# Attention scores as three products over 64 rows for the two heads of a query tile, in place of two products over 128 rows for one head

## The chip, the cores and the metric

The kernel runs on one core of a Trainium2 chip. The metric is the device time of one execution in microseconds; less is better.

## The reference, cut to what matters

A two-layer encoder over 1,280 tokens (1,024 of one sequence, 256 of another), width 1,024, in float32. Each layer projects the normed input, mixes tokens in three ways, projects back, and runs a SwiGLU network. The change touches only the scores of the two attentions: six heads of 64 with a dilated mask over all keys of the sequence, and four heads of 64 with a neighbourhood window and a bias.

```python
qd = to_bhsd(rope(heads(q_d, N_DIL_HEADS), pos))        # dilated: 6 heads of 64
kd = to_bhsd(rope(heads(k_d, N_DIL_HEADS), pos))
...
scores = jnp.einsum('bhrnqe,bhrnke->bhrnqk', qr, kw,
                    preferred_element_type=jnp.float32) * (hd ** -0.5)
...
scores = jnp.einsum('bhrcqe,bhrcke->bhrcqk', qg, kg,    # neighbourhood: 4 heads of 64
                    preferred_element_type=jnp.float32) * (hd ** -0.5)
scores = scores + bias[None].astype(jnp.float32)
```

## The kernel before

Products are made in a rounded 32-bit format (fp32r). To keep float32 accuracy every operand is split into a high part, which is the value rounded, and a low part, which is the value less its high part. A product of two operands is then high by high, high by low and low by high (`products`, L1607 to L1609).

Each layer has five attention blocks of two heads (three dilated, `b` 0 to 2, then two of neighbourhood, `b` 3 and 4). A block first projects k, q and v for its two heads (128 columns: head 0 in partitions 0 to 63, head 1 in 64 to 127), in three chunks of 512, 512 and 256 tokens. VectorE takes k and q from PSUM into `TB` and `TA` (`drain`), in the dilated blocks ScalarE and VectorE rotate them (`swap`, `rope`), and then they are split: ScalarE writes the high parts (`split_k`, `split_q`), VectorE the low parts (`low_k`, `low_q`). Dilated blocks also project three convolution groups: the one named "c" before attention, drained by VectorE into `TA` only after the splits have been queued, and "h" and "b" in pieces between the steps of attention (`convolution`, units 0 to 11).

Because a head has only 64 rows and the array has 128, the kernel stacks the high part of a head's queries on its low part: `QS[0]` holds high in rows 0 to 63 and low in rows 64 to 127, `QS[1]` the reverse. `KH[h]` and `KL[h]` hold the head's keys, high and low, in both halves. Two products over 128 rows (L1720, L1721) then give all four partial products of a head. Writing both halves costs four pieces of 64 partitions per chunk for `KH`, four for `KL`, and two for each part of the queries.

The attention of a block runs over 20 units, two heads for each of ten query tiles of 128. A unit is a head, a query tile and `nkt` key tiles: 8 for the first sixteen units of a dilated block, 4 or 5 for those of a neighbourhood block, 2 for the last four of each. Its scores lie in two PSUM banks, `2 * (u % 2)` and the next. TensorE's program, in order: wait for the last splits and for the drain of the last projection, `scores(0)`, `scores(1)`, `turn_v`, and then for each unit `turn(u)` (transposes of the probabilities), `scores(u + 2)`, half of the convolution piece, `turn_y` after every second unit, the other half, and `values(u - 1)` (16 products of 128 columns for eight key tiles). VectorE adds the mask and takes the maximum (`mask`, L1317), ScalarE takes the exponential (`exp`, L893), and after `turn` they split the turned probabilities (`PTH`, `PTL`). The order on every engine is written out by hand; semaphores hold it together. The one that matters here is `s_masked`: `scores(u + 2)` writes the banks that `mask(u)` reads and waits for it.

Of the kernel before, what the change touches and what calls it, by code (L numbers as in the profile page):

```python
# [7 lines left out]
F32 = mybir.dt.float32  # L8
F32R = mybir.dt.float32r
# [3 lines left out]
P = 128  # L13
# [302 lines left out]
def build(nc, xt, w_in, w_out, w_gate, w_up, w_down, gains, conv_w, rpb, tables, small, mixed,  # L316
          parked, out):
    with ExitStack() as ctx:
# [35 lines left out]
        QS = [place(f"QS{h}", [P, T], F32R, offset=base + 5120 * h) for h in range(2)]  # L354
        KH = [place(f"KH{h}", [P, T], F32R, offset=base + 10240 + 5120 * h) for h in range(2)]
        KL = [place(f"KL{h}", [P, T], F32R, offset=base + 20480 + 5120 * h) for h in range(2)]
# [431 lines left out]
        def _(act):  # L788
# [70 lines left out]
            def split_k(L, b, c):  # L859
# [5 lines left out]
                for h in range(2):  # L865
                    own = TB[64 * h:64 * h + 64, span(c)]
                    for half in (h, 1 - h):
                        ins = nc.scalar.activation(KH[h][64 * half:64 * half + 64, span(c)], own, ACT.Copy)
                ins.then_inc(s_stack_hi, STACK_HI.step((L, "k", b, c)))

            def split_q(L, b, c):
                ready(L, "q", b, c)
                nc.scalar.activation(QS[0][0:64, span(c)], TA[0:64, span(c)], ACT.Copy)
                nc.scalar.activation(QS[1][64:128, span(c)], TA[64:128, span(c)], ACT.Copy) \
                    .then_inc(s_stack_hi, STACK_HI.step((L, "q", b, c)))
# [308 lines left out]
        def _(dve):  # L1184
# [93 lines left out]
            def low_k(L, b, c):  # L1278
                dve.wait_ge(s_stack_hi, STACK_HI[L, "k", b, c])
                for h in range(2):  # L1280
                    own = slice(64 * h, 64 * h + 64)
                    for half in (h, 1 - h):
                        ins = nc.vector.tensor_tensor(KL[h][64 * half:64 * half + 64, span(c)],
                                                      TB[own, span(c)], KH[h][own, span(c)].bitcast(F32),
                                                      ALU.subtract)
                ins.then_inc(s_stack_lo, STACK_LO.step((L, "k", b, c)))

            def low_q(L, b, c):
                dve.wait_ge(s_stack_hi, STACK_HI[L, "q", b, c])
                nc.vector.tensor_tensor(QS[0][64:128, span(c)], TA[0:64, span(c)],  # L1290
                                        QS[0][0:64, span(c)].bitcast(F32), ALU.subtract)
                nc.vector.tensor_tensor(QS[1][0:64, span(c)], TA[64:128, span(c)],
                                        QS[1][64:128, span(c)].bitcast(F32), ALU.subtract) \
# [684 lines left out]
```

## Time and profile before

| | us |
|---|---|
| median of 3 runs | 3647.01 (3646.38 to 3648.12) |
| the profiled execution, its time | 3651.52 |
| the profiled execution, its span | 3649.7 |
| PE busy | 3427.7 (94%) |
| DVE busy | 1515.4 (42%) |
| ACT busy | 1187.5 (33%) |
| mean granted clock of TensorE | 0.959 |

PE is TensorE's matmul row, DVE VectorE, ACT ScalarE. Matmuls overlap at their ends, so a step on PE is read from start to start, not from the length of a row. The profile's span starts a little after the time of the execution does; the difference is 1.8 us.

### The profile page before, as it was taken

Reading aid. Unit: us, or ns where it says so; the run is one execution under the profiler, and the core shown is the slowest. Engines: PE = TensorE matmul, PEld = TensorE weight load, DVE = VectorE, ACT = ScalarE, POOL = GpSimd, SP = SyncE. Lnnn points to the kernel's source line nnn. Section 1 sums busy time; section 2 is a strip of 40 time slices with the busy share of each in tenths; the row PEclk is TensorE's granted clock in tenths of the full one; section 3 lists DMA queues with packets and bytes.
Section 4 is the critical chain, followed back from the end, with each engine's and each line's share of the span. In section 5 each row is a group of like instructions: output and inputs, shape, how many; then the busy total and the mean of one; then the engine's idle time right before and its main releaser. Section 6 shows DMA issues by size and latency. Waiting matters only on the chain. (4 is left out here: it accounts for less than half of the span.)

```text
span 3649.7 us, 45391 instructions
## 1 busy us (share of the span) xinstructions
PE 3427.7 (94%) x18616; PEld 2948.5 (81%) x18616; DVE 1515.4 (42%) x2886; ACT 1187.5 (33%) x2276; POOL 881.1 (24%) x541
## 2 busy tenths in 40 slices
PE   7899998997999999999869999988989999999997
PEld 5878887776888888888768788877868888888886
DVE  4545445525222333322565454555152233332225
ACT  5445444634111111111454454446341111111112
POOL 4101010325222222222421010103242223222223
PEclk8999999999999999999989999999999999999998
DMA  3010111212111111111310100112121111111112
GB/s 126 15 41 13 38 37 35 85 50 107 47 41 35 41 35 35 35 47 35 123 64 12 38 20 31 43 30 96 51 96 52 36 41 35 35 35 47 35 35 116
DMA packets 43343, 179.69 MB, mean 49 GB/s; under 512 B 5376, under 2 KB 7296, under 8 KB 39552
## 3 DMA queue, kind: packets, MB, share of 16 engines
q1 hardware_dynamic: 41120, 167.60, 13.4%
q10 hardware_dynamic: 2016, 9.18, 0.6%
q8 instruction: 149, 2.44, 0.3%
q14 instruction: 58, 0.48, 0.0%
HBM read 146.61 MB, written 30.15 MB: 48 GB/s over the span
## 5 line engine op out<-in xcount | busy, mean ns | idle before, releaser
L1607 PE MATMUL PS<-XH,WH 128*128 128x512 f32 (+1 forms) x3648 | 1324.1, 363 | 23.3 <-DVE XL L1223 13.4
L1608 PE MATMUL PS<-XL,WH 128*128 128x512 f32 (+1 forms) x3648 | 1314.0, 360 | 0.0
L1609 PE MATMUL PS<-XH,WL 128*128 128x512 f32 (+1 forms) x3648 | 1312.8, 360 | 0.0
L1607 PEld LDWEIGHTS PS<-XH,WH 128*128 128x128 f32 x3648 | 704.6, 193 | 129.8 <-POOL WL L651 14.0
L651 POOL TENSOR_TENSOR WL<-RAW,WH 128x1024 fp32r<-128x1024 f32 x196 | 469.8, 2416 | 1313.2 <-ACT WH L792 1313.2
L1608 PEld LDWEIGHTS PS<-XL,WH 128*128 128x128 f32 x3648 | 703.7, 193 | 102.0
L1609 PEld LDWEIGHTS PS<-XH,WL 128*128 128x128 f32 x3648 | 701.7, 192 | 102.9
L667 POOL TENSOR_TENSOR SG<-SG,RS 128x512 f32<-128x512 f32 x132 | 146.7, 1111 | 1039.2 <-ACT SG L959 1039.2
L1401 DVE TENSOR_TENSOR ACC<-ACC,PS 128x512 f32<-128x512 f32 (+1 forms) x480 | 286.7, 599 | 251.9 <-PE PS L1609 250.2
L1607 PE MATMUL PS<-HH,WH 128*128 128x512 f32 (+1 forms) x1056 | 379.3, 359 | 12.0 <-DVE ACC L1401 10.0
L959 ACT ACTIVATE SG<-SG 128x512 f32<-128x512 f32 x132 | 74.0, 561 | 972.1 <-DVE SG L1379 971.7
L1609 PE MATMUL PS<-HH,WL 128*128 128x512 f32 (+1 forms) x1056 | 381.6, 361 | 0.0
L1608 PE MATMUL PS<-HL,WH 128*128 128x512 f32 (+1 forms) x1056 | 379.5, 359 | 0.0
L1753 PE MATMUL PS<-V,PTH 128*128 128x128 f32 x1136 | 280.0, 286 | 25.3 <-issue 14.7
L1754 PE MATMUL PS<-V,PTL 128*128 128x128 f32 x1136 | 281.6, 288 | 0.0
L1379 DVE TENSOR_TENSOR SG<-PS,RS 128x512 f32<-128x512 f32 x132 | 79.5, 602 | 449.5 <-PE PS L1609 445.8
L1753 PEld LDWEIGHTS PS<-V,PTH 128*128 128x128 f32 x1136 | 231.4, 204 | 41.7 <-issue 22.3
L1385 DVE TENSOR_TENSOR HF<-PS,SG 128x512 f32<-128x512 f32 x132 | 79.5, 602 | 410.6 <-PE PS L1609 389.7
L1607 PEld LDWEIGHTS PS<-HH,WH 128*128 128x128 f32 x1056 | 200.6, 190 | 45.3 <-DVE ACC L1401 11.8
L1754 PEld LDWEIGHTS PS<-V,PTL 128*128 128x128 f32 x1136 | 232.1, 204 | 2.6
L1350 DVE TENSOR_TENSOR PTL<-PS,PTH 128x512 fp32r<-128x512 f32 (+1 forms) x328 | 191.1, 615 | 100.7 <-ACT PTH L925 98.5
L964 ACT ACTIVATE HH<-HF 128x512 fp32r<-128x512 f32 x132 | 74.0, 560 | 478.2 <-DVE HF L1385 478.2
(105 smaller groups left out, 3594.6 us busy)
## 6 DMA issues: line engine op xcount, KB each, us to landing
RAW<-w_in SPq DMA_DIRECT2D x48, 512.0 KB, 3.6
RAW<-w_gate SPq DMA_DIRECT2D x44, 512.0 KB, 3.6
RAW<-w_up SPq DMA_DIRECT2D x44, 512.0 KB, 3.6
RAW<-w_down SPq DMA_DIRECT2D x44, 512.0 KB, 3.7
X<-parked SPq DMA_DIRECT2D x6, 2048.0 KB, 7.2
RAW<-w_out SPq DMA_DIRECT2D x16, 512.0 KB, 3.7
parked<-YO SPq DMA_DIRECT2D x4, 2048.0 KB, 6.3
mixed<-YB ACTq DMA_DIRECT2D x8, 640.0 KB, 3.1
```

The costliest lines, as they stand in the source:

```text
L651: nc.gpsimd.tensor_tensor(WL[s][:, :, :], RAW[s][:, :, :], WH[s][:, :, :].bitcast(F32), ALU.subtract).then_inc(s_lo, 1)
L667: nc.gpsimd.tensor_tensor(SG[:, span(c)], SG[:, span(c)], RS[:, span(c)], ALU.mult) \
L959: nc.scalar.activation(SG[:, span(c)], SG[:, span(c)], ACT.Silu) \
L1350: nc.vector.tensor_tensor(PTL[u % 2][:, g, 0:n, :].rearrange("p t q -> p (t q)"), PS[:, 4 + g, 0:n * P], high.bitcast(F32), ALU.subtract) \
L1379: nc.vector.tensor_tensor(SG[:, span(c)], PS[:, bank_of(L, "g", f, c), 0:CHUNKS[c][1]], RS[:, span(c)], ALU.mult).then_inc(s_gate, GATE.st ...
L1385: nc.vector.tensor_tensor(HF[f % 2][:, span(c)], PS[:, bank_of(L, "u", f, c), 0:CHUNKS[c][1]], SG[:, span(c)], ALU.mult).then_inc(s_h, HID ...
L1401: ins = nc.vector.tensor_tensor(ACC[c][:, k, :], ACC[c][:, k, :], ps, ALU.add)
L1607: nc.tensor.matmul(out, wh, xh, start=first, stop=False)
L1608: nc.tensor.matmul(out, wh, xl, start=False, stop=False)
L1609: return nc.tensor.matmul(out, wl, xh, start=False, stop=last)
L1753: nc.tensor.matmul(o, PTH[u % 2][:, g, j, :], v, start=a + j == 0, stop=False)
L1754: last = nc.tensor.matmul(o, PTL[u % 2][:, g, j, :], v, start=False, stop=a + j == nkt - 1)
```

## The change

Queries and keys are split once, over all 128 partitions, with no copies in the other half: `QH`, `QL`, `KH`, `KL`. `scores` now takes a pair of units, the two heads of a query tile. For each group of up to four key tiles it issues six products over 64 rows: high by high for head 0 (partitions 0 to 63) and for head 1 (64 to 127), then low keys by high queries for both, then high keys by low queries for both. Head 0 writes banks 0 and 1, head 1 banks 2 and 3. A pair is issued after every even unit's `turn`, where before each unit issued its own two units ahead, and it waits for the masks of both units of the pair before it. Line numbers after the edits shift: L1607 to L1609 are L1596 to L1598, L1720 and L1721 are L1710, L1732 is L1724, L1753 and L1754 are L1745 and L1746, L1317 is L1306.

```diff
-        QS = [place(f"QS{h}", [P, T], F32R, offset=base + 5120 * h) for h in range(2)]
-        KH = [place(f"KH{h}", [P, T], F32R, offset=base + 10240 + 5120 * h) for h in range(2)]
-        KL = [place(f"KL{h}", [P, T], F32R, offset=base + 20480 + 5120 * h) for h in range(2)]
+        QH = place("QH", [P, T], F32R, offset=base)
+        QL = place("QL", [P, T], F32R, offset=base + 5120)
+        KH = place("KH", [P, T], F32R, offset=base + 10240)
+        KL = place("KL", [P, T], F32R, offset=base + 15360)
...
-                for h in range(2):
-                    own = TB[64 * h:64 * h + 64, span(c)]
-                    for half in (h, 1 - h):
-                        ins = nc.scalar.activation(KH[h][64 * half:64 * half + 64, span(c)], own, ACT.Copy)
-                ins.then_inc(s_stack_hi, STACK_HI.step((L, "k", b, c)))
+                nc.scalar.activation(KH[:, span(c)], TB[:, span(c)], ACT.Copy) \
+                    .then_inc(s_stack_hi, STACK_HI.step((L, "k", b, c)))
...
-                nc.scalar.activation(QS[0][0:64, span(c)], TA[0:64, span(c)], ACT.Copy)
-                nc.scalar.activation(QS[1][64:128, span(c)], TA[64:128, span(c)], ACT.Copy) \
+                nc.scalar.activation(QH[:, span(c)], TA[:, span(c)], ACT.Copy) \
                     .then_inc(s_stack_hi, STACK_HI.step((L, "q", b, c)))
...
-                for h in range(2):
-                    own = slice(64 * h, 64 * h + 64)
-                    for half in (h, 1 - h):
-                        ins = nc.vector.tensor_tensor(KL[h][64 * half:64 * half + 64, span(c)],
-                                                      TB[own, span(c)], KH[h][own, span(c)].bitcast(F32),
-                                                      ALU.subtract)
-                ins.then_inc(s_stack_lo, STACK_LO.step((L, "k", b, c)))
+                nc.vector.tensor_tensor(KL[:, span(c)], TB[:, span(c)], KH[:, span(c)].bitcast(F32),
+                                        ALU.subtract).then_inc(s_stack_lo, STACK_LO.step((L, "k", b, c)))
...
-                def scores(u):
-
-                    i, h, k0, nkt = units[u]
-                    if u >= 2:
-                        pe.wait_ge(s_masked, first + u - 1)
-                    q = QS[h][:, i * P:(i + 1) * P]
+                def scores(pair):
+
+                    i, _, k0, nkt = units[2 * pair]
+                    if pair:
+                        pe.wait_ge(s_masked, first + 2 * pair)
                     for a, n in quads(nkt):
                         keys = slice((k0 + a) * P, (k0 + a + n) * P)
-                        bank = PS[:, 2 * (u % 2) + a // 4, 0:n * P]
-                        nc.tensor.matmul(bank, q, KH[h][:, keys], start=True, stop=False)
-                        last = nc.tensor.matmul(bank, q, KL[h][:, keys], start=False, stop=True)
-                    last.then_inc(s_scored, 1)
+                        for m, (q, k) in enumerate(((QH, KH), (QH, KL), (QL, KH))):
+                            for h in range(2):
+                                own = slice(HD * h, HD * h + HD)
+                                last = nc.tensor.matmul(PS[:, 2 * h + a // 4, 0:n * P],
+                                                        q[own, i * P:(i + 1) * P], k[own, keys],
+                                                        start=m == 0, stop=m == 2)
+                                if m == 2 and a + n == nkt:
+                                    last.then_inc(s_scored, 1)
...
                 scores(0)
-                scores(1)
                 turn_v(nb)
                 for u in range(NU):
                     turn(u)
...
-                    if u + 2 < NU:
-                        scores(u + 2)
+                    if u % 2 == 0 and u + 2 < NU:
+                        scores(u // 2 + 1)
```

Three places in the program show how rows move. The first is PE at unit 0 of the first dilated block: two transposing rows (`EYE,PR`), the scores, and the first convolution products (`XH,WH`). Before:

```order
L1732 MATMUL PS<-EYE,PR 128x128 [waits exped]
L1732 MATMUL PS<-EYE,PR 128x128 x7
L1720 MATMUL PS<-KH_96,QS_94 128x512 [waits masked,vl]
L1721 MATMUL PS<-KL_98,QS_94 128x512
L1720 MATMUL PS<-KH_96,QS_94 128x512
L1721 MATMUL PS<-KL_98,QS_94 128x512
L1607 MATMUL PS<-XH_49,WH_67 128x512 [waits lo]
```

The same place after:

```order
L1724 MATMUL PS<-EYE,PR 128x128 [waits exped]
L1724 MATMUL PS<-EYE,PR 128x128 x7
L1710 MATMUL PS<-KH,QH 128x512 [waits masked,vl]
L1710 MATMUL PS<-KH,QH 128x512
L1710 MATMUL PS<-KL,QH 128x512 x2
L1710 MATMUL PS<-KH,QL 128x512 x2
L1710 MATMUL PS<-KH,QH 128x512 x2
L1710 MATMUL PS<-KL,QH 128x512 x2
L1710 MATMUL PS<-KH,QL 128x512 x2
L1596 MATMUL PS<-XH_49,WH_67 128x512 [waits lo]
```

Where four products of one head stood, twelve of two heads stand, and the four that stood behind the next unit's transposes are gone from there. The wait for `masked` was for unit 0's mask and is now for unit 1's.

The second is PE in a neighbourhood block, at an even unit of five key tiles, down to the first product with the values (`V,PTH`). Before:

```order
L1732 MATMUL PS<-EYE,PR 128x128 [waits ptl,exped]
L1732 MATMUL PS<-EYE,PR 128x128 x4
L1720 MATMUL PS<-KH_96,QS_94 128x512 [waits masked]
L1721 MATMUL PS<-KL_98,QS_94 128x512
L1720 MATMUL PS<-KH_96,QS_94 128x128
L1721 MATMUL PS<-KL_98,QS_94 128x128
L1753 MATMUL PS<-V,PTH_103 128x128 [waits ptl,yb,y]
```

The same place after:

```order
L1724 MATMUL PS<-EYE,PR 128x128 [waits ptl,exped]
L1724 MATMUL PS<-EYE,PR 128x128 x4
L1710 MATMUL PS<-KH,QH 128x512 [waits masked]
L1710 MATMUL PS<-KH,QH 128x512
L1710 MATMUL PS<-KL,QH 128x512 x2
L1710 MATMUL PS<-KH,QL 128x512 x2
L1710 MATMUL PS<-KH,QH 128x128 x2
L1710 MATMUL PS<-KL,QH 128x128 x2
L1710 MATMUL PS<-KH,QL 128x128 x2
L1745 MATMUL PS<-V,PTH_101 128x128 [waits ptl,yb,y]
```

Here six products of 512 columns and six of 128 stand for two and two, and the odd unit after it has none.

The third is DVE in the first block of a layer, from the split of chunk 1 to the drains of the convolution group into `TA`, on which TensorE waits before `scores(0)`. Before:

```order
L1283 TENSOR_TENSOR KL_98<-TB,KH_96 64x512 [waits stack_hi]
L1283 TENSOR_TENSOR KL_98<-TB,KH_96 64x512
L1283 TENSOR_TENSOR KL_99<-TB,KH_97 64x512 x2
L1290 TENSOR_TENSOR QS_94<-TA,QS_94 64x512 [waits stack_hi]
L1292 TENSOR_TENSOR QS_95<-TA,QS_95 64x512
L1283 TENSOR_TENSOR KL_98<-TB,KH_96 64x256 [waits stack_hi]
L1283 TENSOR_TENSOR KL_98<-TB,KH_96 64x256
L1283 TENSOR_TENSOR KL_99<-TB,KH_97 64x256 x2
L1290 TENSOR_TENSOR QS_94<-TA,QS_94 64x256 [waits stack_hi]
L1292 TENSOR_TENSOR QS_95<-TA,QS_95 64x256
L1260 TENSOR_TENSOR TA<-PS,RS 128x512 [waits group,stack_lo]
```

The same place after:

```order
L1277 TENSOR_TENSOR KL<-TB,KH 128x512 [waits stack_hi]
L1282 TENSOR_TENSOR QL<-TA,QH 128x512 [waits stack_hi]
L1277 TENSOR_TENSOR KL<-TB,KH 128x256 [waits stack_hi]
L1282 TENSOR_TENSOR QL<-TA,QH 128x256 [waits stack_hi]
L1257 TENSOR_TENSOR TA<-PS,RS 128x512 [waits group,stack_lo]
```

Twelve splitting instructions ahead of the drain become four.

## Rows read from the trace of the kernel before

**Rows 1.** The page's head and PE's row: busy us, share of the span, instructions
```profile
span 3649.7 us, 45391 instructions
...
PE 3427.7 (94%) x18616; PEld 2948.5 (81%) x18616; DVE 1515.4 (42%) x2886; ACT 1187.5 (33%) x2276; POOL 881.1 (24%) x541
```

**Rows 2.** Groups by line and form: count, busy us, mean ns, idle before
```profile
L1720 PE MATMUL PS<-KH,QS 128*128 128x512 f32 x256 | 119.9, 468 | 25.1 <-DVE TA L1260 21.6 <-DVE YB L1260 2.4 <-DVE V L1300 0.9
...
L1388 DVE TENSOR_TENSOR HL<-HF,HH 128x512 fp32r<-128x512 f32 x88 | 61.6, 700 | 61.4 <-ACT HH L964 61.4
...
L1283 DVE TENSOR_TENSOR KL<-TB,KH 64x512 fp32r<-64x512 f32 x80 | 54.8, 685 | 17.7 <-ACT KH L868 16.9
```

**Rows 3.** Windows: dilated block, neighbourhood block, start of the second layer's first block
```profile
core 0: us, PE busy (x) PEld busy (x) DVE busy (x) ACT busy (x) POOL busy (x), PEclk, DMA share, GB/s
275.00:285.00 10.00, 10.00 (x59) 8.57 (x58) 5.80 (x15) 5.23 (x9) 2.38 (x1) 1.00 0.00 1
600.00:615.00 15.00, 14.06 (x112) 12.90 (x110) 10.94 (x36) 12.40 (x35) 4.75 (x2) 1.00 0.01 1
1920.00:1935.00 15.00, 11.17 (x36) 8.96 (x37) 7.57 (x17) 7.15 (x11) 1.21 (x1) 0.61 0.00 0
```

**Rows 4.** Timeline of PE, dilated block: start us, us, engine, line, operation
```profile
152.78 1.06 PE L1732 MATMUL PS<-EYE,PR 128*128 128x128 f32 x8
153.60 0.48 PE L1720 MATMUL PS<-KH,QS 128*128 128x512 f32 x1
153.92 0.40 PE L1721 MATMUL PS<-KL,QS 128*128 128x512 f32 x1
...
154.62 0.39 PE L1607 MATMUL PS<-XH,WH 128*128 128x512 f32 x1
```

**Rows 5.** Timeline of all engines, first block of the second layer
```profile
1904.26 0.76 DVE L1233 TENSOR_TENSOR TAB<-TAB,RS 128x256 f32<-128x256 f32 x2
...
1909.76 2.55 ACT L868 ACTIVATE KH<-TB 64x512 fp32r<-64x512 f32 x4
...
1919.21 1.62 DVE L1260 TENSOR_TENSOR TA<-PS,RS 128x512 f32<-128x512 f32 x3
...
1920.97 0.77 PE L1720 MATMUL PS<-KH,QS 128*128 128x512 f32 x1 [12.37 <-DVE TA L1260]
...
1929.04 1.97 PE L1732 MATMUL PS<-EYE,PR 128*128 128x128 f32 x8 [1.88 <-ACT PR L893]
```

**Rows 6.** Timeline of all engines, first block of the first layer
```profile
94.91 0.28 PE L1609 MATMUL PS<-XH,WL 128*128 128x256 f32 x1
...
101.97 0.76 PE L1720 MATMUL PS<-KH,QS 128*128 128x512 f32 x1 [6.77 <-DVE TA L1260]
...
107.30 1.28 ACT L893 ACT_TABLE_LOAD   x1
```

**Rows 7.** Timeline of all engines, start of the second dilated block
```profile
269.23 0.47 PE L1720 MATMUL PS<-KH,QS 128*128 128x512 f32 x1 [0.61 <-DVE TA L1260]
...
274.04 1.09 PE L1732 MATMUL PS<-EYE,PR 128*128 128x128 f32 x8 [0.45 <-ACT PR L893]
...
274.63 1.22 DVE L1317 CUSTOM_DVE_ANT_0 PR<-PS,TAB 128x1024 f32<-128x1024 f32 x1
...
274.89 0.48 PE L1720 MATMUL PS<-KH,QS 128*128 128x512 f32 x1
```

**Rows 8.** Timeline of PE, neighbourhood block, units of five key tiles
```profile
593.79 0.77 PE L1732 MATMUL PS<-EYE,PR 128*128 128x128 f32 x5 [0.73 <-ACT PR L893]
594.31 0.48 PE L1720 MATMUL PS<-KH,QS 128*128 128x512 f32 x1
...
595.03 0.28 PE L1753 MATMUL PS<-V,PTH 128*128 128x128 f32 x1
...
596.15 0.74 PE L1732 MATMUL PS<-EYE,PR 128*128 128x128 f32 x5
...
601.58 0.74 PE L1732 MATMUL PS<-EYE,PR 128*128 128x128 f32 x5 [0.21 <-ACT PR L893]
```

More of the change, by code:

```diff
@@ L1279, in low_k @@
                 dve.wait_ge(s_stack_hi, STACK_HI[L, "k", b, c])
-                for h in range(2):
-                    own = slice(64 * h, 64 * h + 64)
-                    for half in (h, 1 - h):
-                        ins = nc.vector.tensor_tensor(KL[h][64 * half:64 * half + 64, span(c)],
-                                                      TB[own, span(c)], KH[h][own, span(c)].bitcast(F32),
-                                                      ALU.subtract)
-                ins.then_inc(s_stack_lo, STACK_LO.step((L, "k", b, c)))
+                nc.vector.tensor_tensor(KL[:, span(c)], TB[:, span(c)], KH[:, span(c)].bitcast(F32),
+                                        ALU.subtract).then_inc(s_stack_lo, STACK_LO.step((L, "k", b, c)))
             def low_q(L, b, c):
                 dve.wait_ge(s_stack_hi, STACK_HI[L, "q", b, c])
[L1290 to L1293, printed above, removed]
-                    .then_inc(s_stack_lo, STACK_LO.step((L, "q", b, c)))
+                nc.vector.tensor_tensor(QL[:, span(c)], TA[:, span(c)], QH[:, span(c)].bitcast(F32),
+                                        ALU.subtract).then_inc(s_stack_lo, STACK_LO.step((L, "q", b, c)))
             def split_v(nb):
```

## The prediction

> **What bounds the kernel now.** I read the page's head first: TensorE is busy for 94% of the span [rows 1], so a change of its program pays or costs directly wherever it does not wait. The grouped lines say how much the scores are: 256 products L1720 of 512 columns and as many L1721, and the only large idle time in front of them, 25.1 us, is mostly a wait for `TA`, the drain behind the splits [rows 2]. Next the windows, by stage. In a dilated block PE is busy 10.00 of 10.00 us while VectorE and ScalarE have 5.80 and 5.23: pure PE bound. In a neighbourhood block PE has 14.06 of 15, ScalarE 12.40: PE and the loop through the exponential are nearly even [rows 3]. Last, the timelines of the first block of each layer, where PE stands still for 6.77 and 12.37 us before the first scores, because VectorE is still splitting [rows 5, 6]. So there are three stages with three different limits, and the change touches each.
>
> **The idle time at the first block.** In the second layer VectorE begins the tables of chunk 2 at 1904.26, behind the splits of chunk 0; ScalarE's four key pieces of chunk 1 run from 1909.76; VectorE works without a break until the drain at 1919.21, and PE starts at 1920.97 [rows 5]. A piece over 64 partitions costs 685 ns, a subtraction of 512 columns over 128 partitions 700 [rows 2]: the price is per instruction, so four for one saves three quarters. Chunk 0: 4 + 2 pieces of VectorE become 1 + 1, 4.2 us becomes 1.4, and ScalarE's four key pieces ahead of them (2.55 in chunk 1) become one of 0.7, so they could begin 1.9 earlier; I take 1.3, because the rotation of q has to end first. The tables move up by 4.1. The rest moves with them, so chunk 1 can be split from about 1905.6. From there: 1.0 for the last rotation, 2 x 0.69 and 2 x 0.42 for four subtractions, then drain to start of PE as now, 1.76 (1919.21 to 1920.97). PE starts at 1910.6, 10.4 earlier; it ended the convolution products at 1908.60 (1920.97 less 12.37), so that is possible. In the first layer the same shortening is cut off by PE's own end: 94.91 + 0.28 = 95.19, then the drain of the last chunk, which elsewhere leaves 0.61 of idle time [rows 7]. PE starts at 95.8 for 101.97: 6.2. Together 16.6 us. Without the moving up of the tables the second layer gives 6.3 alone and both 12. Blocks further on have 0.61 and nothing to win.
>
> The clock goes with it: after such a standstill the granted clock over 15 us is 0.61 [rows 3], that is long stretches at 1.2 GHz. From first scores to first transposes it takes 8.07 there [rows 5] and 4.81 in the second block at full clock [rows 7], of which 1.28 is a table load that only the first blocks have [rows 6]: 2.0 are the clock. The later wait for the exponential stays and may drop it again, so I count 3 us for both layers, with 0 and 10 as ends.
>
> **The products, dilated blocks.** Four products of a unit take from 153.60 to 154.62, 1.02 us: 0.32 for the first step behind the transposes, 0.23 for each other [rows 4]. A pair now costs 2.04. After, twelve products stand for eight. The trace has no product over 64 rows, so I bound it. If head 0's and head 1's product run side by side (their rows, weights and PSUM banks are apart): 0.32 + 5 x 0.23 = 1.49, 0.55 less. If they run one after the other: 0.32 + 11 x 0.23 = 2.88, 0.84 more. Between them lies a cost for changing from 128 rows to 64 and back. Its nearest row: a product lasts 0.39 while the next starts after 0.23 [rows 4], so waiting until the array is empty costs about 0.17 at each change, of which the first step already pays 0.09 (0.32 less 0.23); 0 to 0.25 a pair. I take side by side, since nothing that the two products use is shared, and 0.11 for the changes: 0.44 less a pair. Each dilated block has eight pairs of eight key tiles, the first in the start; 7 x 6 blocks = 42 pairs give 18.5 us, 12.6 to 23.
>
> The Trainium skill (TensorE: Matmul & The Clock Gate, Part 3) says that products in different row groups run concurrently, some 4 ns apart, and reports 3.07 times the speed for four of them; by its span rule these 42 pairs would give the full 23 us and the sum below 3617, which no row here shows.
>
> **The start of a block.** The first pair is as long as before or shorter, but `scores(1)` behind unit 0's transposes now waits for unit 1's mask. That runs from 274.63 to 275.85, while the scores it now holds back started at 274.89 [rows 7]: 1.06 us, in the four dilated blocks that start like this; PE is full behind it, so it is lost. Behind the waiting scores stand the convolution piece and unit 1's transposes. In the first blocks it is 0.2, in the neighbourhood ones I take 0.3: 4.2 + 0.4 + 1.1 = 5.7 us lost. Later on the mask of unit u + 1 is done before the transposes of u are, and costs nothing; the work that hides it is `values`, sixteen products at 0.11 [rows 8], 1.8 us.
>
> **Neighbourhood blocks.** A unit of five key tiles is 0.52 transposes (593.79 to 594.31), 0.72 scores, 1.12 values (ten products, 0.11 each), 2.36 in all and without a wait at its end (596.15); three units take 7.79, 2.60 each, since the others wait for ScalarE [rows 8]. After, an even unit carries the pair: 0.78 for six products of 512 columns side by side, and for six of 128 columns 0.33, or 0.66 if their weight loads follow each other, as the step of 0.11 suggests. That makes 2.75 to 3.08. An odd unit has 1.7 of PE work, less than the 2.7 at which ScalarE lets units follow ((7.79 - 2.36) / 2), so what PE saves there is not had. A pair: 2.9 + 2.7 = 5.6 for 5.2. 16 such pairs lose 6.5 us (0 to 10). With four key tiles it evens out. Pairs of two key tiles: another 1 us.
>
> **Sum.** -16.6 - 3 - 18.5 + 5.7 + 6.5 + 1 = -24.9. The profiled execution took 3651.5, so 3626.6; the median of the runs is 4.5 lower, so 3622. The ends together: 3602 to 3640.
>
> **Rivals.**
> One after the other: the two halves do not run side by side. For it: each product takes a step for its own columns, and none shares a step with another [rows 4, 8]. Against it: only that nothing is shared. Then 42 pairs cost 0.84 each, 35 us; the block starts 17 for 5.7; five-key pairs 0.52 + 2.14 + 1.12 + 2.7 = 6.5 for 5.2, 20 us; four-key pairs 0.55 each, 9; the small ones 5; less 19.6 at the first blocks: 66 us slower, 3712. It decides as soon as a couple of 64-row products takes more than about 0.33 for 0.23. Chance 0.25.
>
> The change of shape is dear: side by side, but each way from 128 to 64 rows and back empties the array and leaves the first weight load bare, 0.17 + 0.19 each. Then a pair gains nothing in the dilated blocks (0.55 less 0.6) and loses 0.5 more in the others, so that only the first blocks' gain remains against 5.7 + 15: 3645 to 3650. For it: the 0.09 that even a change from transposes to products costs. Chance 0.12. The Trainium skill (TensorEngine Tiling (Array Packing), Key Properties) says that changing the tiling mode drains the engine. By that rule the price is the 0.17 each way worked out above; nothing in this trace changes mode.
>
> The clock: products on half the rows, or idle odd units, make the granted clock fall to its lower level in a neighbourhood block. It is at 0.61 around idle time now [rows 3]. A block of twenty units of up to 2.6 us at half clock would cost 15 to 20. Chance 0.03, slower.
>
> **Chances.** The forecast has 0.60. About what a measurement here can tell from no change is 0.2%, 7.3 us: of the forecast all but a sliver lies beyond it; of the dear change of shape two thirds lie within. Faster 0.62, same 0.09, slower 0.29. The range must reach half way into the first rival to leave out no more than two in ten: 3602 to 3712; the forecast's own is 3602 to 3640.
>
> **What would show it.** In the profile after: PE starts the first scores of the two layers about 0.7 and 2 us behind the last convolution product; two score products start nearly together, and the steps of couples are 0.23; from first score to the next stage 1.5 to 1.75 us for twelve products; a wait of about 1 us for the mask behind the first transposes of the dilated blocks; neighbourhood units in turns of about 2.9 and 2.7. If starts lie evenly 0.23 apart, the first rival holds. The prediction is wrong above all if the halves do not run together; next if PE's program at odd units waits longer than I think because its scores no longer fill it.

## The result and the profile after

The changed kernel took 3666.52 us (median of 5 runs, 3655.81 to 3668.39), the kernel before on the same chip 3648.12 (5 runs, 3646.38 to 3649.71). The ratio is 1.0043, 95% interval 1.0032 to 1.0054: slower, by 12 to 20 us. 24.9 us less were forecast. The page of the changed kernel, head and PE's row, beside [rows 1]:

```profile
span 3664.7 us, 45807 instructions
...
PE 3442.5 (94%) x18944; PEld 2931.5 (80%) x18944; DVE 1436.2 (39%) x2766; ACT 1117.9 (31%) x2156; POOL 881.1 (24%) x541
```

VectorE lost 79 us of work and ScalarE 70, as the splits promise; the span grew by 15.0 all the same. The grouped lines say where PE waits for scores (compare [rows 2], where the drain `TA` cost 21.6):

```profile
L1710 PE MATMUL PS<-KH,QH 64*128 64x512 f32 x256 | 63.4, 487 | 14.8 <-DVE STAT L1306 7.0 <-DVE TA L1257 5.4 <-DVE YB L1257 2.4
```

The standstill went from 21.6 to 5.4, and 7.0 of waiting for masks (`STAT`, L1306) are new. First block of each layer, timeline of PE, beside [rows 5, 6] with their 6.77 and 12.37 of idle time:

```profile
96.39 0.49 PE L1710 MATMUL PS<-KH,QH 64*128 64x512 f32 x2 [0.61 <-DVE TA L1257]
...
1920.08 0.49 PE L1710 MATMUL PS<-KH,QH 64*128 64x512 f32 x2 [2.33 <-DVE TA L1257]
```

Now the pair in a dilated block, timeline of PE and of its weight loads (PEld), beside [rows 4]. "x2" is a couple, one product for each head:

```profile
150.73 1.06 PE L1724 MATMUL PS<-EYE,PR 128*128 128x128 f32 x8
...
151.72 0.19 PEld L1710 LDWEIGHTS PS<-KH,QH 64*128 64x128 f32 x2 [0.17 <-issue]
151.73 0.49 PE L1710 MATMUL PS<-KH,QH 64*128 64x512 f32 x2
...
152.06 0.39 PE L1710 MATMUL PS<-KL,QH 64*128 64x512 f32 x2
...
152.99 0.39 PE L1710 MATMUL PS<-KH,QL 64*128 64x512 f32 x2
153.31 0.19 PEld L1596 LDWEIGHTS PS<-XH,WH 128*128 128x128 f32 x1 [0.36 <-issue]
153.31 0.50 PE L1596 MATMUL PS<-XH,WH 128*128 128x512 f32 x1
...
153.65 0.40 PE L1597 MATMUL PS<-XL,WH 128*128 128x512 f32 x1
```

The halves do run side by side: couples step by 0.23. But the weights of the first couple, and of the first convolution product behind the last, are loaded only when the shape before is done (0.17 and 0.36 with nothing to do for the loader). From the transposes' start to the first couple it takes 1.00 us, where it took 0.82 to the first product; from the last couple to the next stage 0.32 for a step of 0.23, and that stage's own first step is 0.34.

Last the windows of the first neighbourhood block (us, PE busy, granted clock, DMA), after and then before:

```profile
566.00:574.00 8.00, 3.62 (x23) 0.78 0.23 66
574.00:598.00 24.00, 23.99 (x114) 0.50 0.01 1
598.00:626.00 28.00, 24.73 (x194) 1.00 0.00 1
```

```profile
575.00:583.00 8.00, 3.97 (x26) 1.00 0.24 66
583.00:591.00 8.00, 7.28 (x34) 0.57 0.00 0
591.00:635.00 44.00, 38.97 (x277) 0.96 0.14 37
```

In both PE is half idle at the start and then at 1.2 GHz. Before, it is back at 2.4 after some 8 us; after, it stays at 1.2 for 24 us in which it never rests. Over the whole run the trace's clock record has 331.5 us at the lower level for 300.1. The time from the first to the last mask of a neighbourhood block, and in brackets what of it, up to 8 us behind the last mask, was at the lower clock (taken here and below from the clock record; the expectations have 50.7 and 92.3 for the two sums, from means rounded to two decimals):

```
us           before        after
layer 1, 3   45.9 (9.9)    54.7 (32.3)
layer 1, 4   48.2 (15.0)   54.2 (24.1)
layer 2, 3   46.0 (9.9)    47.9 (11.4)
layer 2, 4   48.2 (15.0)   54.1 (23.8)
together    188.3 (49.8)  210.9 (91.6)
```

That is +22.6 us, more than the whole loss. Of the ten kernels here that keep the old neighbourhood products and issue nothing in idle time, none has more than 56.2 us in brackets.

### The profile page after: what moved, and what is told of

Read it like the earlier page. It is cut to its first block and busy times, and to the rows that moved or that the text cites. A ratio compares the mean times of both kernels' runs of the same rounds, so it can differ in the third digit from the quotient of the medians.

```text
span 3664.7 us, 45807 instructions
## 1 busy us (share of the span) xinstructions
PE 3442.5 (94%) x18944; PEld 2931.5 (80%) x18944; DVE 1436.2 (39%) x2766; ACT 1117.9 (31%) x2156; POOL 881.1 (24%) x541
## 5 line engine op out<-in xcount | busy, mean ns | idle before, releaser
L1596 PE MATMUL PS<-XH,WH 128*128 128x512 f32 (+1 forms) x3648 | 1331.8, 365 | 23.3 <-DVE XL L1220 13.4
L1598 PE MATMUL PS<-XH,WL 128*128 128x512 f32 (+1 forms) x3648 | 1313.1, 360 | 0.0
L1596 PEld LDWEIGHTS PS<-XH,WH 128*128 128x128 f32 x3648 | 705.5, 193 | 139.6 <-issue 18.6
L1598 PEld LDWEIGHTS PS<-XH,WL 128*128 128x128 f32 x3648 | 702.7, 193 | 103.2
L1596 PE MATMUL PS<-HH,WH 128*128 128x512 f32 (+1 forms) x1056 | 379.0, 359 | 12.4 <-DVE ACC L1390 10.4
L1598 PE MATMUL PS<-HH,WL 128*128 128x512 f32 (+1 forms) x1056 | 381.2, 361 | 0.0
L1745 PE MATMUL PS<-V,PTH 128*128 128x128 f32 x1136 | 287.0, 292 | 29.2 <-issue 18.6
L1746 PE MATMUL PS<-V,PTL 128*128 128x128 f32 x1136 | 285.1, 290 | 0.0
L1745 PEld LDWEIGHTS PS<-V,PTH 128*128 128x128 f32 x1136 | 232.8, 205 | 49.8 <-issue 31.3
L1596 PEld LDWEIGHTS PS<-HH,WH 128*128 128x128 f32 x1056 | 200.4, 190 | 45.7 <-DVE ACC L1390 12.2
L1746 PEld LDWEIGHTS PS<-V,PTL 128*128 128x128 f32 x1136 | 234.7, 207 | 1.7
L1597 PEld LDWEIGHTS PS<-HL,WH 128*128 128x128 f32 x1056 | 200.7, 190 | 33.7
```

Source lines behind the costliest of these rows:

```text
L1596: nc.tensor.matmul(out, wh, xh, start=first, stop=False)
L1597: nc.tensor.matmul(out, wh, xl, start=False, stop=False)
L1598: return nc.tensor.matmul(out, wl, xh, start=False, stop=last)
L1745: nc.tensor.matmul(o, PTH[u % 2][:, g, j, :], v, start=a + j == 0, stop=False)
L1746: last = nc.tensor.matmul(o, PTL[u % 2][:, g, j, :], v, start=False, stop=a + j == nkt - 1)
```

## The experiments

Fifteen kernels in four groups. The kernel before took 3650.98, 3649.70, 3650.28 and 3650.51 us beside them; differences are against these unless another kernel is named. A switch chooses by block whether scores are 64-row products of once-split operands, and whether they come in pairs:

```diff
+                    if b not in ROWS64:
+                        scores_one(2 * pair, False)
+                        scores_one(2 * pair + 1, False)
+                        return
...
+                    if b not in PAIRS:
+                        if u + 2 < NU:
+                            scores_one(u + 2)
```

`scores_one` is the old `scores`, and the old splits go with it. Blocks 0 to 2 are dilated, 3 and 4 neighbourhood.

### Which part of the change, in which blocks

```diff
+ROWS64 = ()
+PAIRS = (0, 1, 2, 3, 4)
```

The new order and waits with the old products. 

> The kernel before with one thing of the change: scores issued in pairs, with the wait for both masks, but as the old stacked products over 128 rows with the old splits. Theory clock (the products over 64 rows keep the granted clock down in the neighbourhood blocks; of the 22.6 us that the four blocks lost from first to last mask, about 16 are clock): the neighbourhood blocks lose only the order's share, some 2 us each, and the dilated blocks the 1 us at each start, 3648 + 8 + 6 = about 3662, with low clock in the neighbourhood blocks as before (about 34 us in all). Rival order (lumping the scores in every second unit is the cause of it all, the clock follows it): the neighbourhood blocks lose 20 us or more here too, with long low stretches, about 3675.

Measured: 3683.10, ratio 1.0086 (1.0072 to 1.0100), +32, more than either theory expected. The neighbourhood blocks took 198.9 us at no more low clock than before (49.6): +10.6, the order's own price there. These blocks wait for the masks of both units as the changed kernel does (1.17 us of PE at 589.50), so the order and its wait alone do not bring the long stretches at 1.2 GHz. Of the rest 14.9 us lie between the masks of the dilated blocks (585.4 for 570.5). Of these a block with no low clock from first to last mask takes 94.22 us for 92.14, 2.0 of it in its first three intervals; the remainder goes with more low clock.

```diff
+ROWS64 = (0, 1, 2)
+PAIRS = (0, 1, 2)
```

The change in the dilated blocks only. 

> The change in the dilated blocks alone; the neighbourhood blocks keep old splits, old products and old order. Both theories: the four neighbourhood blocks are back at 46 to 48 us from first to last mask, so 22.6 us less than the changed kernel, about 3644, a little faster than before by the standstill saved at the first blocks (13.7 us) less the lost starts. If instead it comes out near 3666, the loss was not in the neighbourhood blocks' own program but in a clock that the dilated blocks hand on.

Measured: 3637.33, ratio 0.9961 (0.9948 to 0.9975), -13.7. This part is a gain, though not the 34 that the forecast's terms give it.

```diff
+ROWS64 = (3, 4)
+PAIRS = (3, 4)
```

The change in the neighbourhood blocks only. 

> The change in the neighbourhood blocks alone. If the loss sits in their own program: 3648 + 22 = about 3670. If the long low clock there depends on when the block begins against the clock's changes (the changed kernel has 27 us low in one block and 7 in its twin of the next layer), the sum of the low stretches differs from 68 us and the time with it: 3655 to 3675.

Measured: 3670.46, ratio 1.0054 (1.0042 to 1.0067), +19.5. The blocks took 203.6 us with 64.6 at the lower clock. Another 4.2 us stand between the first layer's last mask and the second's first (1200.8 for 1196.6, with 86.4 us of low clock for 73.4), 2.2 behind the last mask of all. So the loss lies here, and the whole change is worse than its parts' sum (-13.7 + 19.5 = +6 for +12 to +20): block 3 of the first layer had 8.2 us of low clock in this kernel and 32.3 in the changed one.

```diff
+ROWS64 = (0,)
+PAIRS = (0,)
```

The change in the first block of each layer. 

> The change in the first block of each layer only; the four other dilated blocks and the neighbourhood blocks are as before the change. If what the change gains is the standstill of the two first blocks (6.0 and 8.7 us seen) and a dilated block's pairs gain only 0.09 us each against a start that loses 1: 4 x (1.0 - 0.6) = 1.6 faster than 3637.33, near 3635.5. Rival: side-by-side products are worth the 0.44 us a pair that was forecast: 4 x (3.1 - 1.0) = 8 slower, near 3646.

Measured: 3632.05, ratio 0.9951 (0.9939 to 0.9963), -17.7. Its first mask stands at 96.53 us in the first layer (104.19 before); from the last mask of the first layer to the first of the second it is 1185.5 for 1196.6.

```diff
+ROWS64 = (1, 2)
+PAIRS = (1, 2)
```

The other dilated blocks. 

> The change in the second and third block of each layer only. With the change in all dilated blocks 3637.33 us, in the first ones only 3632.05: if the parts add up, these four blocks cost 5 us, near 3655, all of it at the blocks' starts (1.0 us each for the wait for mask(1)) and in the clock. Rival: the 5 us is the scatter of those runs and the pairs gain their 0.09 us: 3648 to 3650, no difference.

Measured: 3650.48, ratio 0.9999 (0.9991 to 1.0008): nothing. So all that the dilated part gains is the standstill of the two first blocks; 28 pairs elsewhere win no more than four starts lose. In truth they win less: where such a block has no low clock from first to last mask it takes 93.0 us for 92.1 before, and that the run's time did not grow goes with the clock, which was low for 272.8 us in this trace and for 300.1 before. -17.7 and 0 add up to somewhat more than the -13.7 of both; the clock's share moves that much between kernels (below).

### What the 64-row products cost

```diff
+            for i in range(2 * N):
+                half = (low, high)[i % 2]
+                last = nc.tensor.matmul(PS[:, 2 * (i % 2), :], XR[half, 0:P], XR[half, 512:1024], start=True, stop=True)
```

Series of products on one operand, a rest between them; it computes nothing of the reference. 

> Another program that computes none of the reference (its outputs are filled with zeros and one PSUM row): after idle stretches of some 10 us, seven stretches of products: 96 of 128 rows and 512 columns; 96 of 64 rows on one half; 192 of 64 rows on the halves in turn; 192 of 128 rows and 128 columns; 384 of 64 rows and 128 columns in turn; then groups of twelve 64-row products in turn with six 128-row ones between; and the same with six on one half, then six on the other. Theory clock: the granted clock rises later or never in the stretches over 64 rows on one half, and perhaps with 128 columns. Rival order: it rises in all of them alike. Steps: 0.23 for a couple of 512 columns; the weight loads decide the 128-column couples, 0.11 if side by side and 0.21 if one after the other; each change of shape costs about 0.2; products of one half in a row cost 0.23 each.

Measured, groups by line; L65 128 rows, L70 64 rows on one half, L76 64 rows in turn, L81 and L87 the same as L65 and L76 over 128 columns, L94 and L103 twelve 64-row products in turn and by halves, between six of 128 rows (one execution, each series once):

```profile
L70 PE MATMUL PS<-XR 64*128 64x512 f32 x96 | 41.3, 630 | 6.4 <-DVE T L52 6.4
L87 PE MATMUL PS<-XR 64*128 64x128 f32 x384 | 41.2, 412 | 6.4 <-DVE T L52 6.4
L81 PE MATMUL PS<-XR 128*128 128x128 f32 x192 | 41.2, 415 | 6.4 <-DVE T L52 6.4
L103 PE MATMUL PS<-XR 64*128 64x512 f32 x144 | 28.5, 428 | 6.4 <-DVE T L52 6.4
L76 PE MATMUL PS<-XR 64*128 64x512 f32 x192 | 24.2, 414 | 6.4 <-DVE T L52 6.4
L65 PE MATMUL PS<-XR 128*128 128x512 f32 x96 | 24.0, 414 | 17.8 <-DVE T L52 17.8
L94 PE MATMUL PS<-XR 64*128 64x512 f32 x144 | 21.2, 429 | 6.4 <-DVE T L52 6.4
```

A couple of 64 rows costs what one product of 128 does (24.2 us for 96 couples, 24.0 for 96 products). And the price of a visit: in the section in turn, at 2.4 GHz,

```profile
233.45 1.66 PE L94 MATMUL PS<-XR 64*128 64x512 f32 x12
235.04 1.66 PE L96 MATMUL PS<-XR 128*128 128x512 f32 x6
236.64 1.66 PE L94 MATMUL PS<-XR 64*128 64x512 f32 x12
```

six couples and six products take 3.19 us, and twelve steps of 0.227, as products of L65 follow each other at that clock, would take 2.72: 0.46 a visit, half of it at each change. And the clock: windows with L70, L76, L81 and L87, and with L94; in the first the clock is still at 2.4 GHz for a part of the rest.

```profile
40.00:82.00 42.00, 35.63 (x87) 0.57 0.00 0
...
98.00:100.00 2.00, 2.00 (x12) 0.50 0.00 0
104.00:112.00 8.00, 8.00 (x74) 1.00 0.00 0
...
152.00:195.00 43.00, 36.63 (x272) 0.50 0.00 1
196.00:221.00 25.00, 19.23 (x182) 0.50 0.00 1
222.00:265.00 43.00, 40.20 (x216) 0.94 0.00 1
```

Behind a rest, the products on one half alone and both series over 128 columns ran 41 us at 1.2 GHz without a pause and the clock did not rise; in the series of 512 columns over the whole array, as one product or as a couple, it came up within 5 us. So idle time before a series does not settle its clock. The stretch at 0.50 of the neighbourhood block has much work of the former kind (transposes and values, 128 columns each).

```diff
-                        scores(u // 2 + 1)
+                        split = u < 12 and b in DIL
+                        scores(u // 2 + 1, 0 if split else None)
...
+                    if b in PAIRS and u % 2 == 0 and u < 12 and b in DIL:
+                        scores(u // 2 + 1, 1)
```

One more change of shape in 36 pairs. 

> The change in the dilated blocks only, and for units 0 to 10 of a block the three couples on the second four key tiles stand behind half a convolution piece: one more stretch of 64-row products for each of 36 pairs, with the same products. If a change of shape and back costs what the trace after shows (0.47 us, of which 0.1 to 0.2 was paid before it as ordinary starts): +0.3 to +0.4 x 36 = +11 to +14, near 3650. Rival: shape costs only the first step of a stretch (0.08 to 0.11 us): +4, near 3641.

Measured: 3662.89, +25.6 against the dilated change. In the second dilated block the first 13 intervals between masks took 74.7 us for 72.2: 2.5 for six pairs, 0.42 each, what one more visit to the other shape costs; 36 of them are 15, a little over what was expected. The other 11 were not expected. This block lost 3.3 us more in its last two intervals and had more low clock (16.7 us for 7.5).

```diff
-                        for m, (q, k) in enumerate(((QH, KH), (QH, KL), (QL, KH))):
-                            for h in range(2):
+                        for h in range(2):
+                            for m, (q, k) in enumerate(((QH, KH), (QH, KL), (QL, KH))):
```

Three products of head 0, then three of head 1. 

> The change in the dilated blocks only, with the same six products of a group ordered by head: three of head 0 on one half, then three of head 1 on the other. If a couple overlaps only when the halves alternate: four of six products have no neighbour on the other half, a group takes about 1.2 us more at the worst and 0.5 at the least (one meeting of halves is left), two groups x 42 pairs: +40 to +85 if TensorE were the only bound, less where VectorE is: 3665 to 3700. Rival: TensorE reaches the other half's product past the queue anyway, or these stretches wait for VectorE: within 5 of 3637.

Measured: 3636.51 (6 runs, 3627.73 to 3647.03), ratio 0.9962 (0.9948 to 0.9975): no difference to 3637.33. The trace has the same six couples 0.23 apart: TensorE starts a product of the free half past three that stand before it. Then six and six, the loop over heads outermost. 

> The change in the dilated blocks only, with all six 64-row products of head 0 (both groups of four key tiles) ahead of the six of head 1. Ordered by three the trace still showed couples, so TensorE took a product of the other half from behind three. If it does not take one from behind six: the microkernel's groups of six and six took 28.5 us for 21.2 of 16 groups in turn, 0.46 a group, so 42 pairs x 0.46 = +19, near 3656; that is then what running side by side is worth here. Rival: it takes them from behind six too, or these stretches wait for others: within 5 of 3637.

Measured: 3678.82, +41.5 against the dilated change, twice what was expected. Its pair, timeline of PE:

```profile
157.26 0.49 PE L1760 MATMUL PS<-KH,QH 64*128 64x512 f32 x1
...
157.83 0.39 PE L1760 MATMUL PS<-KH,QL 64*128 64x512 f32 x1
157.84 0.61 PE L1760 MATMUL PS<-KH,QH 64*128 64x512 f32 x2
158.18 0.50 PE L1760 MATMUL PS<-KL,QH 64*128 64x512 f32 x2
158.41 0.51 PE L1760 MATMUL PS<-KH,QL 64*128 64x512 f32 x2
158.64 0.39 PE L1760 MATMUL PS<-KH,QH 64*128 64x512 f32 x1
...
159.10 0.39 PE L1760 MATMUL PS<-KH,QL 64*128 64x512 f32 x1
159.43 0.50 PE L1629 MATMUL PS<-XH,WH 128*128 128x512 f32 x1
```

Three alone, three couples, three alone: nine steps for six, 2.17 us for 1.58. It looks past three and not past six. (The microkernel's section has twelve groups, not the sixteen of the expectation: 0.61 a group, which is this pair's 0.59.) 42 x 0.59 = 25 of the 41.5; two dilated blocks also had 20.7 us of low clock for 7. At the same low clock the second dilated block took 97.7 us for 93.2. So three couples taken apart cost 0.6 us a pair: that much at least running side by side is worth, far more than the change saves in a pair.

### The start of a block

```diff
                     elif u % 2 == 0 and u + 2 < NU:
+                        if u == 0 and beside is not None:
+                            beside(0, 0)
                         scores(u // 2 + 1)
-                    if beside is not None:
+                    if beside is not None and not (u == 0 and b in PAIRS):
                         beside(u, 0)
```

> The change in the dilated blocks only, as in the kernel that took 3637.33 us, and at unit 0 of each dilated block half of the first convolution piece stands ahead of the second pair's scores, which wait for mask(1). If that wait is what a block's start lost (the first three intervals of masks took 11.6 us for 10.6), it is covered: about -1 us in each of six blocks, near 3632. Rival: the wait only moves, since what follows the scores (transposes, values) is then late by as much: near 3637.

Measured: 3639.54 (12 runs, 3632.83 to 3650.48), ratio 0.9977 (0.9967 to 0.9987): inconclusive, no gain in the median and wide scatter. The first three intervals of the second dilated block took 10.7 us for 11.6 in the profiled runs, so the wait itself is covered, and that execution took 3632.98, near the 3632 expected; the median does not show it. With the first blocks only. 

> The change in the first block of each layer only (3632.05 us), and half a convolution piece ahead of the second pair's scores there. It covers the wait for mask(1), about 1 us in each of two blocks: near 3630. Rival: the block's length follows from where the clock falls in it (94.8 us with 11.5 us at the lower clock, 99.0 with 21.1), which a piece moved ahead may change by up to 4 us a block: 3624 to 3640.

Measured: 3627.72 (5 runs, 3626.68 to 3629.76), ratio 0.9938 (0.9926 to 0.9950), -22.6: faster than both kernels, and the fastest here. Its first block took 95.0 us with 10.8 at the lower clock, for 99.0 with 22.3 in the kernel without the piece moved ahead; so part of these 4 us is the clock, as the rival said.

### The clock in the neighbourhood blocks

```diff
+                    if b not in DIL and pair == 0:
+                        for _ in range(8):
+                            for h in range(2):
+                                own = slice(HD * h, HD * h + HD)
+                                nc.tensor.matmul(PS[:, 2 * h, 0:4 * P], QH[own, 0:P], KH[own, 0:4 * P],
+                                                 start=True, stop=True)
```

The whole change, and products without use where PE would wait. 

> The whole change (3666.52 us), and ahead of the first pair's scores of each neighbourhood block 16 more 64-row products over 512 columns (8 couples) into a bank that the scores then overwrite. They do no work of the result; at the lower clock they take 8 x 0.43 = 3.4 us a block. If the 20 us and more at the lower clock at the start of three of the four blocks come from what TensorE is given there (a stretch of 512-column products raised the clock in the microkernel, 128-column ones did not), the clock rises after them and each of the three blocks gets 5 to 10 us back: 3666.5 + 4 x 3.4 - 3 x 10 = 3650. Rival: the clock stays as it is: near 3680.

Measured: 3644.47 (12 runs, 3634.36 to 3675.53), ratio 0.9992 (0.9974 to 1.0010), -22.0 against the changed kernel's 3666.52. The start of its first neighbourhood block, timeline of PE and windows:

```profile
570.77 2.11 PE L1709 MATMUL PS<-KH,QH 64*128 64x512 f32 x16 [0.61 <-DVE YB L1257]
572.67 0.44 PE L1716 MATMUL PS<-KH,QH 64*128 64x512 f32 x2
...
577.82 0.75 PE L1716 MATMUL PS<-KH,QH 64*128 64x512 f32 x2 [1.15 <-DVE STAT L1306]
```

```profile
574.00:578.00 4.00, 1.68 (x14) 0.99 0.00 0
578.00:582.00 4.00, 3.80 (x19) 0.59 0.00 0
582.00:586.00 4.00, 3.73 (x32) 1.00 0.01 4
```

They ran at the high clock, 2.1 us a block for the 3.4 counted, and cost nothing: the gap between the blocks' masks is 55.5 us with and without them. The clock now falls at about 578 and is back within 4 us; the four blocks took 197.0 us (37.2 low) for 210.9 (91.6). Three of them gained; block 3 of the second layer had more low clock than without (18.7 us for 11.4). The 12 runs scatter over 41 us, so the 22.0 is good to some 6 us. How much of the 22 would any kernel gain?

```diff
+                if b not in DIL:
+                    for _ in range(8):
+                        nc.tensor.matmul(PS[:, 0, 0:4 * P], QS[0][:, 0:P], KH[0][:, 0:4 * P],
+                                         start=True, stop=True)
```

The kernel before, with such products. 

> The kernel before, with 8 products of 128 rows and 512 columns ahead of the first scores of each neighbourhood block, which do no work of the result and overwrite a bank that the scores then fill. The blocks of before spend 50.7 us at the lower clock. If such products hold the clock up here as in the changed kernel (92.3 to 37.9 us), these blocks too lose some 20 to 30 us of it, worth up to half: 3638 to 3645. Rival, that only the changed kernel's stretches are helped: 3650.

Measured: 3643.61 (11 runs, 3638.06 to 3651.89), ratio 0.9986 (0.9977 to 0.9995), -6.9; blocks 180.7 us (24.6 low). Then the change in the neighbourhood blocks only, with them. 

> The change in the neighbourhood blocks only (3670.46 us), with the same idle-time products as couples of 64 rows. With the clock held up the order alone is left: its price was 10.6 us in the kernel with pairs and old products. So near e13_before_warm + 10: about 3650. Rival: if the new products are themselves dearer there (three for two in a group of 128 columns), +15 to +20.

Measured: 3657.76 (11 runs, 3655.02 to 3676.65), ratio 1.0025 (1.0015 to 1.0035), -12.7 against the same kernel without them; blocks 192.9 us (29.8 low). So with the clock held up about alike, the change costs 14.2 us there by the medians, 12.2 by the traces; expected were 10, or 15 to 20.

Is that the order or the products? The seventh and the nineteenth mask of the second neighbourhood block, timeline of DVE, in stretches with no low clock: the kernel before with idle-time products, the kernel with old products in pairs, the whole change with idle-time products.

```profile
2500.49 0.81 DVE L1317 CUSTOM_DVE_ANT_0 PR<-PS,IB 128x640 f32<-128x640 f32 x1
...
2530.28 0.41 DVE L1317 CUSTOM_DVE_ANT_0 PR<-PS,EB 128x256 f32<-128x256 f32 x1
```

```profile
703.88 0.82 DVE L1339 CUSTOM_DVE_ANT_0 PR<-PS,IB 128x640 f32<-128x640 f32 x1
...
736.31 0.41 DVE L1339 CUSTOM_DVE_ANT_0 PR<-PS,EB 128x256 f32<-128x256 f32 x1
```

```profile
2502.41 0.81 DVE L1306 CUSTOM_DVE_ANT_0 PR<-PS,IB 128x640 f32<-128x640 f32 x1
...
2535.00 0.41 DVE L1306 CUSTOM_DVE_ANT_0 PR<-PS,EB 128x256 f32<-128x256 f32 x1
```

29.79, 32.43 and 32.59 us; in the first neighbourhood block the same stretch takes 28.5, 30.2 and 30.4. The order costs 2.6 and 1.7 us, the 64-row products 0.2. And the fastest kernel with idle-time products. 

> The change in the first blocks only with the convolution piece ahead (3627.72 us), and the idle-time products of e13_before_warm in the neighbourhood blocks. If parts add up, it gains what e13_before_warm gains over the kernel before (5 to 12 us): 3616 to 3623. Rival: 3628.

Measured: 3629.57 (5 runs, 3626.51 to 3632.20), ratio 0.9943 (0.9930 to 0.9955): the rival, no gain on 3627.72. Its blocks 3 and 4 of the first layer kept 45.9 and 48.1 us (9.9 and 11.5 low), those of the second had 44.7 and 45.8, and the two first blocks were 3 us longer each at more low clock (19.8 and 22.4 us). What such products bring depends on where the clock happens to stand when they come.

## Why the prediction was wrong

By medians: the dilated part -13.7, the neighbourhood part +14.2 with the clock held up, together about 0, as the two kernels with idle-time products say directly (3644.47 and 3643.61, +0.9); and of the 22.0 us that these products give back to the changed kernel, 6.9 they give to the old one too. The other 15 are what the change costs through the clock, which makes +16. The 15 is a difference of medians of scattered runs. The traces give some 12: with no low clock from first to last mask the changed program takes 46.5 us for the first neighbourhood block and 48.9 for the second, so of the 210.9 at most 20.2 are the clock; the old program's four took 180.7 with idle-time products for 188.3 without, so at least 7.6 of those were.

- **The idle time at the first block: right.** 6.2 and 10.4 were forecast. PE's first scores stand at 96.39 (-5.6) and the first mask 6.0 us earlier; the second layer's came up by a further 7.7 (changed kernel) to 11.1 (change in first blocks only); the stretch between the layers' masks has 75.1 us of low clock in the one and 62.3 in the other, so a part of the difference is the clock. That kernel's -17.7 stands for the forecast -16.6, but it holds 2.9 us by which its second first block was shorter at less low clock, and so near a hit is luck.
- **The clock goes with it, -3: wrong.** The first blocks took 94.8 to 99.5 us in kernels with the change there, the one in six and six aside (95.3 and 98.9 in the changed one), and 94.2 to 99.3 in kernels with the old program there. No steady gain.
- **The products, dilated blocks: the mechanism right, a term mis-sized.** Side by side is right to 0.01: six steps, 0.33 and 0.23. But the change of shape costs 0.18 ahead of the first couple, 0.09 behind the last and 0.11 in the next stage's first step, and the odd unit's next stage now pays the 0.08 of its own that scores paid before: 0.46, where I took 0.11 with 0.25 as the end. The pair takes 1.49 + 0.46 = 1.95 for 2.04: 0.09 saved, 4 us for 42 pairs instead of 18.5. The masks of a block's middle, at full clock, say how little of it is left: fourth to sixteenth mask 69.34 us before, 69.62 with old products in pairs, 69.13 after. The products win 0.08 a pair, the order takes 0.05 of it back. I had looked for the price in how the array empties; the trace shows that the next weights are not loaded ahead across a change of shape, on either side. The forecast's second rival named this with 0.17 + 0.19 each way, a price somewhat too high, and had the dilated pairs nearly right. The microkernel's 0.46 a visit and the 0.42 of one more visit agree with the 0.46 here. The Trainium skill (TensorEngine Tiling (Array Packing), Key Properties) says that a change of tiling mode drains the engine. The trace agrees: the loader stands idle for 0.17 and 0.36 us around the 64-row products. (The forecast's "below 3617", for the full 23 us, comes to 3617.5 by its own terms.)
- **The start of a block: right.** PE waited 0.87 for mask(1) at 265.87, and the first three intervals of masks took 11.6 us for 10.6, for 1.06 forecast. (The rows named there, 275.85 less 274.89, give 0.96; that the slip agrees to the hundredth is luck.) It eats what the pairs gain.
- **Neighbourhood blocks: too cheap.** 6.5 and some 2 for starts and small pairs were forecast, 12.2 to 14.2 found with the clock held up, 10.6 in the kernel with the old products. The 128-column products are as I took them at best (0.06 and 0.11 apart), but pairs of five-key units took 0.6 us more, not 0.4: in the second neighbourhood block of the first layer three of them had 6.0, 5.9 and 6.5 us, in the kernel with idle-time products, for 5.4, 5.2 and 5.8 before. Here the price is the order's and not that of bare weight loads: the kernel with old products in pairs has 6.0, 5.9 and 6.5 too. The second rival, which has the change of shape cost 0.5 a pair in these blocks, is wrong there. The forecast's last sentence, that PE's program at odd units may wait longer than I think, fits: in the kernel with idle-time products PE waits 0.32 and 0.85 us for `PR` at 2499.99 and 2505.94. How the order's price divides among such waits was not worked out.
- **The clock, a chance of 0.03: this decided.** The mechanism was on my list, with 15 to 20 us as its price, and 12 to 15 were found; in the sum it stood at nothing. I gave it no weight because the block before fell to 1.2 GHz too and came back. The step that failed is there, together with the 14 us too much for the dilated pairs: I had only counted the idle time that brings the clock down, and the time until it comes back is not the same after the change (27.3 us at a stretch in the first neighbourhood block, for 6.8 before). The kernel with old products in pairs has the same order and the same wait for masks and only 49.6 us of low clock, so neither is enough without the 64-row products. Why it stays low with them is open. The microkernel's series behind like rests show that work without a pause can leave it at 1.2 GHz, but no run varied this in the block itself.

Not settled: why block 3 of the second layer kept 11.4 us of low clock where the other three had 24 to 32, in the same code. The clock's share is set by where in a stretch it falls, and that moved between kernels by 4 us a block without any edit there.

## What to carry to other kernels

Products on two row halves do run side by side at the price of one, but a visit to another array shape cost 0.42 to 0.46 us here; go there for a long stretch or not at all. Price a new order of the same products by itself: here it took 10.6 us in the neighbourhood blocks. Test a change block by block: here the same edit gained 18 us in two blocks, nothing in four and lost 20 in four others. And read the granted clock of a stretch beside its busy share: PE busy 23.99 of 24.00 at 0.50 is half a TensorE. A few idle-time products of 512 columns ahead of it gave 22, 13 and 7 us in three kernels here and nothing in a fourth.

## What the hardware showed that I had not expected

- TensorE takes a product for the free row half past three that wait for the other (couples at 0.23 in both orders), and not past six (three alone, three couples, three alone).
- In one execution of the microkernel, 96 products of 64 rows on one half, 192 of 128 rows over 128 columns, and 384 of 64 rows in turn over 128 columns each took 41 us at 1.2 GHz behind a rest, without a pause and without a rise; 96 couples over 512 columns took 24.2.
- Weight loads stand back at a change of array shape: 0.17 and 0.36 us idle in the loader's rows around a stretch of 64-row products, where the kernel before has none around its scores.
